# A down-projection as seven block products, each summed wholly in PSUM, in place of tile-by-tile sums in SBUF

## The reference, cut to what matters

```python
hn = rms_norm(h, ffn_norm_w)
g, val = jnp.split(hn @ w_up, [D_FF], axis=-1)
g_conv = causal_dwconv(g_hist, ffn_conv_w) + ffn_conv_b
y = h + (jax.nn.silu(g_conv) * val) @ w_down
```

## Time and profile before

| what | us |
|---|---|
| median of 3 runs | 1752.43 |
| lowest, highest | 1752.2, 1753.86 |
| span of the profiled execution | 1750.6 |
| down-projection, first to last matmul start | 1497.7 to 1746.6 |

### The profile page before, as it was taken

One profiled execution on the slowest core, in us unless ns is written; L12 is line 12 of the kernel. 1 busy time (PEld: TensorE's weight loads), 2 busy tenths in 40 slices (PEclk: granted clock), 3 DMA queues, 4 the chain that ended last, 5 costly groups with the idle time before them and its releaser, 6 DMA issues.

```text
span 1750.6 us, 31893 instructions
## 1 busy us (share of the span) xinstructions
PE 1683.5 (96%) x11519; PEld 1618.8 (92%) x11519; DVE 1242.1 (71%) x1957; ACT 695.0 (40%) x1054; POOL 881.0 (50%) x466
## 2 busy tenths in 40 slices
PE   7999999999999989999799998999999999999999
PEld 5858999999999878889799998999999999999999
DVE  5569999999899645565543378877677776655555
ACT  4755552232111377776212335434444444211110
POOL 2504762455786556664221225766666666733331
PEclk9999999999999889999999999999999999999999
DMA  5321112111776242322343312222222222622222
GB/s 197 84 70 37 36 48 86 61 49 61 267 236 207 75 140 77 87 85 85 110 135 132 143 64 80 88 75 83 72 77 79 72 94 86 231 97 96 96 77 97
DMA packets 66978, 178.32 MB, mean 102 GB/s; under 512 B 15386, under 2 KB 15514, under 8 KB 66762
## 3 DMA queue, kind: packets, MB, share of 16 engines
q1 hardware_dynamic: 56786, 140.91, 24.3%
q10 hardware_dynamic: 9392, 32.10, 4.8%
q0 software_dynamic: 720, 4.29, 0.6%
HBM read 141.79 MB, written 35.58 MB: 101 GB/s over the span
## 4 chain that ended last, share of the span: by engine, by line
PE 76%; DVE 11%; ACT 3%; POOL 3%; issue 3%; SPq 2%; DMA 1%; DVEq 0%; ACTq 0%; POOLq 0%
PE PS L667 17%; PE PS L1079 15%; PE PS L1143 11%; PE PX L1079 6%; PE PS L1002 5%; PE PS L1047 5%; PE PS L955 4%; PE PX L1143 4%; PE PS L925 2%; DVE S L2158 2%; DVE M L2156 2%; PE PX L938 2%; PE PS L983 2%; DVE LD L2138 2%; PE PS L770 1%
## 5 line engine op out<-in xcount | busy, mean ns | idle before, releaser
L667 PE MATMUL PS<-XH,WHI 128*128 128x346 f32 (+1 forms) x984 | 322.1, 327 | 5.8 <-POOL WLO L1778 4.5
L667 PE MATMUL PS<-XL,WHI 128*128 128x346 f32 (+1 forms) x984 | 318.6, 324 | 0.0
L667 PE MATMUL PS<-XH,WLO 128*128 128x346 f32 (+1 forms) x984 | 318.0, 323 | 0.0
L1778 POOL TENSOR_TENSOR WLO<-WRAW,WHI 128x1024 fp32r<-128x1024 f32 x58 | 143.4, 2472 | 296.8 <-ACT WHI L1171 296.7
L2158 DVE MATCH_REPLACE8 S<-M,S 128x1024 f32<-128x1024 f32 (+3 forms) x224 | 206.1, 927 | 0.0
L667 PEld LDWEIGHTS PS<-XH,WHI 128*128 128x128 f32 x984 | 186.9, 190 | 15.7 <-issue 8.8
L2156 DVE MAX8 M<-S 128x8 f32<-128x1024 f32 (+3 forms) x224 | 200.8, 932 | 0.4
L667 PEld LDWEIGHTS PS<-XL,WHI 128*128 128x128 f32 x984 | 187.1, 190 | 0.0
L667 PEld LDWEIGHTS PS<-XH,WLO 128*128 128x128 f32 x984 | 187.1, 190 | 0.0
L2432 DVE TENSOR_TENSOR HY<-HY,PS 128x344 f32<-128x344 f32 x198 | 100.9, 514 | 79.2 <-PE PS L1143 79.2
L1143 PE MATMUL PS<-FH,DLO 128*128 128x344 f32 x396 | 126.7, 320 | 0.0
(11 more groups left out here) (369 smaller groups left out, 4818.5 us busy)
## 6 DMA issues: line engine op xcount, KB each, us to landing
WRAW<-wtiles SPq DMA_DIRECT2D x49, 512.0 KB, 3.7
KR<-cache_k SPq DMA_DIRECT2D x64, 256.0 KB, 3.1
RING<-cache_v SPq DMA_DIRECT2D x64, 256.0 KB, 3.0
ffn_act<-TG ACTq DMA_DIRECT2D x22, 516.0 KB, 2.7
FRAW<-ffn_act SPq DMA_DIRECT2D x11, 1032.0 KB, 7.0
RAWG<-wtiles SPq DMA_DIRECT2D x22, 512.0 KB, 3.7
RAWV<-wtiles SPq DMA_DIRECT2D x22, 512.0 KB, 4.4
DRAW<-wdown SPq DMA_DIRECT2D x11, 1024.0 KB, 4.9
```

What stands on the lines that cost most here:

```text
L667: last = nc.tensor.matmul(PS[b][:, c, 0:n], w[b][:, kk, :], x[:, kk, t0 + c * n:t0 + (c + 1) * n], start=(kk == 0 and p == 0), stop=(kk == ...
L1778: nc.gpsimd.tensor_tensor(WLO[b][:, :, :], WRAW[b][:, :, :], WHI[b][:, :, :].bitcast(F32), ALU.subtract).then_inc(w_lo[b], 1)
```

## The change

The down-projection is now seven block products as well. Both halves of the hidden width (11 tiles each, k = 0 to 10), both halves of the 1032 rows (516 columns, as 2 x 258) and both halves of the 8 output tiles make 2x2 blocks. The order of the products is `GROUPS`; step n = 11 g + k is one tile of one product, 77 in all.

- SP loads all 22 activation tiles once into `KA` and `KB` (528 KB each, `ACTS` groups them by semaphore), the weights in 99 quarters of 128x512 (256 KB) into eight buffers `WQ` in turn, and the residual into `HY`, in one written-out order. Quarter j waits until the low part of the step that used quarter j - 8 is done. P5 takes three quarters a step, P7 two, P6 none, the others one.
- ScalarE casts per step the activation half (`x_high`, after TensorE finished step n - 3) and the weights (`w_high`). GpSimd makes all weights' low parts (`LOW_POOL` = 77), VectorE the activations' (`x_low`), and VectorE also the sums of weights (two per step of P5, kept in `S2`; one for P3 and P7) two steps ahead, and the sums of activations T1 to T4 (11 each).
- TensorE keeps the sum of a product over its 11 steps in PSUM, four pairs of banks. At the first step of a product each pair waits for VectorE's add of the product before it (`add_product`, at position 11 g + 1 of VectorE's order, the last thing there); P5 is copied from PSUM to SBUF by ScalarE first (`keep_p5`) and used twice. P6, P7 and P4 go on in the banks without a restart.
- The last tile's work of the up-projection lies among the first steps. The PSUM banks of the up-projection are laid out anew; its products are the same.

```diff
-        FRAW = [at("FRAW0", [P, 2, NY], oh1 + 8192), at("FRAW1", [P, 2, NY], o7 + 2 * HB)]
-        DRAW = at("DRAW", [P, 2, D], oh1)
+        KA = at("KA", [P, KS, NY], oh1)
+        KB = at("KB", [P, KS, NY], o7)
+        S2 = at("S2", [P, KS, 512], oh1 + 4 * KS * NY)
...
+        GROUPS = ("P2", "P5", "P3", "P1", "P6", "P7", "P4")
+        STEPS = KS * len(GROUPS)
+        PARTS = {"P2": ((0, 0),), "P5": ((0, 1), (KS, 1), (KS, 0)), "P3": ((0, 0),), "P1": ((KS, 0),), "P6": (),
+                 "P7": ((KS, 1), (KS, 0)), "P4": ((0, 1),)}
+        LOW_POOL = STEPS
...
+            def quarter(j):
+                n, f, h = QUARTERS[j]
+                if j >= 8:
+                    sp.wait_ge(*low_ready(QUARTERS[j - 8][0]))
+                sp.dma_start(WQ[j % 8][:, :], wd_d[f, :, h * 512:(h + 1) * 512]).then_inc(quarter_in(j)[0], 16)
...
+            for p, js, fs in (("P1", (0, 1), (0, 1, 2, 3)), ("P5", (2,), (4, 5, 6, 7)), ("P6", (3,), ()), ("P2", (4, 5), ()),
+                              ("P7", (6, 7), ()), ("P3", (), (8, 9, 10)), ("P4", (), ())):
+                sp.wait_ge(mm[1], place(NF // 2 - 1, 1, p))
...
+            for j, fs in ((8, (11, 12)), (9, (13, 14)), (10, (15, 16)), (11, (17, 18)), (12, (19, 20)), (13, (21,))):
+                quarter(j)
+                for f in fs:
+                    activation(f)
+            for x in range(2):
+                for j in range(14 + 3 * x, 17 + 3 * x):
+                    quarter(j)
+                for m in range(4 * x, 4 * x + 4):
+                    residual_back(m)
+            for j in range(20, len(QUARTERS)):
+                quarter(j)
...
+            def down(n):
+                g, k, r = n // KS, n % KS, n % 3
+                pe.wait_ge(d_xl, n + 1)
+                pe.wait_ge(*low_ready(n))
+                new = GROUPS[g] in ("P2", "P5", "P3", "P1")
+                for m in range(4):
...
+                    elif k == 0:
+                        pe.wait_ge(*((d_p5, m + 2) if GROUPS[g - 1] == "P5" else (d_add, 4 * (g - 1) + m + 1)))
+                    for q, (w, x) in enumerate(((DWH[r], DXH[r]), (DWH[r], DXL[r]), (DWL[r], DXH[r]))):
+                        for c in range(2):
+                            last = nc.tensor.matmul(PAIRS[m][:, c, :], w[:, m * P:(m + 1) * P], x[:, c * YQ:(c + 1) * YQ],
+                                                    start=new and k == 0 and q == 0, stop=k == KS - 1 and q == 2,
+                                                    skip_group_check=True)
...
+            for n in range(7, STEPS):
+                x_high(n)
+                w_high(n)
+                if n == 2 * KS + 1:
+                    for m in range(4):
+                        keep_p5(m)
...
-            def act_low(i, b):
-                pool.wait_ge(f_hi, i + 1)
-                nc.gpsimd.tensor_tensor(FL[b][:, :, :], FRAW[b][:, :, :], FH[b][:, :, :].bitcast(F32), ALU.subtract).then_inc(f_lo, 1)
+            def w_low(n):
+                pool.wait_ge(d_wh, n + 1)
+                nc.gpsimd.tensor_tensor(DWL[n % 3][:, :], w_source(n), DWH[n % 3][:, :].bitcast(F32),
+                                        ALU.subtract).then_inc(d_wlp, 1)
...
+            def weight_sums(n):
+                for j in js:
+                    dve.wait_ge(*quarter_in(j))
+                if g == "P5":
+                    nc.vector.tensor_tensor(w[1], w[0], w[1], ALU.add).then_inc(d_sum, 1)
+                    dve.wait_ge(d_sum, w_sums(n) - 1)
+                    nc.vector.tensor_tensor(S2[:, k, :], w[1], w[2], ALU.subtract).then_inc(d_sum, 1)
...
+            def position(n):
+                x_low(n)
+                if n >= LOW_POOL:
+                    w_low(n)
+                if n + 2 < STEPS:
+                    weight_sums(n + 2)
+                for what, n0 in (("T1", 6), ("T2", 3 * KS), ("T3", 4 * KS), ("T4", 6 * KS - 2)):
+                    if 0 <= n - n0 < KS:
+                        act_sum(what, n - n0)
+                if n % KS == 1 and n > KS:
+                    add_product(n // KS - 1)
```

More of the change, by code:

```diff
@@ L43 @@
 Y0 = NMETA - C0
[L44 to L45 removed]
+NY = 1032
+YH = NY // 2
+YQ = YH // 2
 NH, HD = 8, 64
@@ L603, in _ @@
                         up_weights(i, a, which)
[L605 to L609, removed]
-            def down_weights(i):
-                sp.dma_start(DRAW[:, :, :], wd_d[ds(2 * i, 2), :, :].rearrange("a p m -> p a m")).then_inc(d_raw, 16)
-            def residual_back(m):
-                sp.dma_start(HY[m][:, :], hx_d[m, :, :]).then_inc(x_in[m], 16)
@@ L630, in _, with activation @@
-            down_weights(1)
-            def down_loads(i, b):
-                sp.wait_ge(f_lo, i - 1)
-                activations(i, b)
-                sp.wait_ge(d_lo, i)
-                down_weights(i)
-            for i in range(2, NF // 2):
-                down_loads(i, i % 2)
+            def activation(f):
+                a, i = f % 2, f // 2
+                sp.wait_ge(slab_out[a], (112, 128)[a] + 16 * (i + 1))
+                t, k = (KA, f) if f < KS else (KB, f - KS)
+                sp.dma_start(t[:, k, :], act_d[f, :, :]).then_inc(acts_in(f)[0], 16)
@@ L1156, in _ @@
+            for n in range(STEPS):
+                down(n)
         @block.scalar
@@ L1988, in _ @@
             times_rms(NF // 2 - 1, 0)
-            act_low(0, 0)
-            weight_low(0, 0)
+            for n in range(5):
+                w_low(n)
             times_rms(NF // 2 - 1, 1)
-            with pool.Fori(0, NF // 4) as j:
-                for b in (1, 0):
-                    act_low(2 * j + 2 - b, b)
-                    weight_low(2 * j + 2 - b, b)
+            for n in range(5, LOW_POOL):
+                w_low(n)
         @block.vector
@@ L2494, in _ @@
             up(NF // 2 - 1, 0)
-            up(NF // 2 - 1, 1, True)
-            conv(NF // 2 - 1, 1)
-            for m in range(KD):
-                dve.wait_ge(x_in[m], 64)
-                down(0, NCH * m, NCH * m + NCH)
-                if m == 2:
-                    times_val(NF // 2 - 1, 1)
-            with dve.Fori(1, NF // 2) as i:
-                down(i)
+            conv(NF // 2 - 1, 0)
+            times_val(NF // 2 - 1, 0)
+            add(NF // 2 - 1, 1, "G1")
+            x_low(0)
+            add(NF // 2 - 1, 1, "V2")
+            x_low(1)
+            add(NF // 2 - 1, 1, "G2")
+            gates(NF // 2 - 1, 1)
+            x_low(2)
+            conv(NF // 2 - 1, 1, lambda: x_low(3))
+            x_low(4)
+            x_low(5)
+            times_val(NF // 2 - 1, 1)
+            for n in range(6, STEPS):
+                position(n)
+            add_product(len(GROUPS) - 1)
 def _constants():
```

245 lines of the change are left out of this document (159 added, 86 removed).

## The result

The changed kernel takes 1756.78 us (median of 18 runs, 1751.63 to 1760.43), the kernel before 1752.87 us (18 runs, 1747.4 to 1757.18). The ratio is 1.0023, 95% interval 1.0014 to 1.0033: **slower by 0.2%**, where 0.5% faster was forecast. The profiled execution took 1759.62 us by itself, with a span of 1757.8.

A forecast was written before the change was run, and what follows sets the result against it. TensorE's down-projection matmuls, running without idle time, were taken as the bound. Terms -28.9 + 11 + 2.5 + 2 + 1 + 3.4 = -9.0 us took 1752.4 to 1743.4 us; own range 1736 to 1750, with rivals 1727 to 1753.

The forecast's parts named there:

- TensorE's work: Down-projection: 1848 matmuls of 258 columns at 119.1 ns take 220.1 us instead of 249.0, so -28.9 us.
- first boundary: P2 to P5: TensorE's step 11 waits for P2's adds, behind sums needing quarters 20 to 22; +11 us (5.4 to 15).
- the clock behind it: After the first boundary's gap TensorE runs 5.4 us at 0.55 of the pace; +2.5 us, bounds 0 and 5.
- P5's own loop: In P5, releasing and reloading a third quarter takes 3.26 us a step against 2.86; +2 us (0 to 8).
- P5 to P3: At step 22 VectorE's eight adds, 4.9 us, and two low parts against two steps of cover; +1 us (0 to 2).
- four other boundaries: At steps 33, 44, 55, 66 VectorE's chain takes 3.8 us against 2.86; 4 x 0.85 = +3.4 us (0.2 to 4).
- the 1537.6 for quarter 22: First boundary: landing time of quarter 22, taken between estimates of 1536.1 and 1538.9 us.
- SP's stop: SP waits before activation 21 until tile 21 is written, by 1514 or so; costs nothing, its queue being behind.
- The rate of the DMA: First boundary: a full DMA moves 409 GB/s by a profile row, preferred to the skill's 358; 3.16 MB take 7.7 us.
- Rival (b): In P5 quarters land late, 6.1 us, making the loop 4.8 us a step; kernel slower at 1760.8 us; chance 0.14.
- The end: After the last matmul: add 0.69 for 0.51 us, half the output bytes in the last transfers; 0 change.
- The chances: Whole kernel: faster by over 0.2% (below 1748.9 us) 0.82, same 0.06, slower 0.12.

The follow-up runs named there:

- e5: Changed kernel with a product's adds right behind x_low at boundaries and P5's second four adds spread over positions 27 to 30; 1740.83 us, 0.9941 of the kernel before.
- e1: Changed kernel with residual rows 4 to 7 loaded behind quarter 45 instead of quarter 19; 1755.28 us, 1.0017 of the kernel before.
- e2: Changed kernel with P2's four adds at VectorE's position 12 ahead of the weight sums for step 14; 1750.08 us, 0.9983 of the kernel before.

## Why the prediction was wrong, point by point

The chain of waits was the forecast's, each pause near where it was named; what failed were three terms of the sum, and all three were forecast too small: the pace of a matmul, the landing of quarter 22 and the adds of P5. The sizes added up to 13.2 us too little. The forecast length is 249.0 - 9.0 = 240.0 us, the measured one 253.2.

| term of the prediction | forecast | measured | off |
|---|---|---|---|
| TensorE's work, 1848 matmuls | 220.1 | 224.7 | +4.6 |
| first boundary | 11 | 14.4 | +3.4 |
| the clock behind it | 2.5 | 2.4 | -0.1 |
| P5's own loop | 2 | 1.9 | -0.1 |
| P5 to P3 | 1 | 5.0 | +4.0 |
| four other boundaries | 3.4 | 3.9 | +0.5 |
| not accounted for | | 0.9 | +0.9 |

- **TensorE's work** failed by the step "so 258 columns take 119.1 ns". It is a slope between two rows of two different stages, carried to a third, and it had no bounds in the sum, although the prediction itself said what 5 ns are worth. A product after a pause took 32.1 us, 121.6 ns by 264. Of that, 120.5 ns are the pace without a pause (e5), 2.6 us over the forecast in 1848; the rest, 2 us, I put down to the refilling behind eight pauses (0.2 each), for which there was no term at all. There is no one pace for a shape to carry over: 260 columns took 119.1 to 120.5 ns in the up-projection, and 258 take 119.5, 120.0 or 121.9 here, by the buffer.
- **The first boundary** was right in place and chain: adds behind sums for step 14 behind quarters 20 to 22. e1 and e2 take away one link each and the pause shrinks by 3.5 and 5.9 us. The step that failed is the 1537.6 for quarter 22, 39.9 us behind the first matmul. It landed 43.9 us behind it (1545.2 against 1501.3), 4.0 later. The 1537.6 is the middle of two estimates, of which the first has only 3.16 MB in front of the quarter. The second counts every byte of the queue, and it was the right one: loads land one behind the other from 1489 on, with no gap. Taking the middle cost 1.3 us. The other 2.5 are the rate: 22.9 MB took from 1484.3, SP's first issue, to 1545.2, less the 2.4 that are not transfer, 58.5 us or 391 GB/s, where the forecast took the 409 of one window of 5 us. The chain behind the landing took 0.2 more (2.9), and step 10 ended 0.8 later than forecast: 3.4. The low part of step 12 did end 1.5 us behind TensorE's last matmul, with sums that had waited for late quarters, and not 0.3 ahead of step 10's end; in a queue with this backlog that moved nothing. At 14.4 the term lies inside its own bounds (5.4 to 15).
- **SP's stop** ahead of activation 21 lasted until 1523.1, not 1514, as the write of tile 21 took 6.5 us to land in the full queue; it cost nothing, as the prediction says, since the loads issued before it went on landing until 1527.6.
- **The rate of the DMA.** The Trainium skill ("SBUF — State Buffer", "A bandwidth-pool intuition that's wrong") has about 358 GB/s between HBM and a core. Here the rows show 390 to 408 for sixty microseconds, so a row was rightly taken in its place, if one that stood at the top of its range.
- **The clock** was right for the first gap: pairs 0.43 us apart for 5.7 us. The bound "with two such gaps, 5" was the case: the pause at step 24 lost another 1.7, counted above with P5 to P3.
- **P5's own loop** was right (0.76, 0.47 and some of 0.1 to 0.2). Rival (b), the slower outcome, forecast 1760.8 with quarters that land late all through P5; the time came near it (1756.8) by another way. By the rows behind 1555 the DMA is at 59% and P5 runs without long pauses, so (b) is refuted as a mechanism. (Its landing for no change is 4.4 us by its own loop, 3.5 + 4.4 over two steps, and not 4.7.)
- **P5 to P3** failed by "two steps of cover". VectorE began its eight adds at 1586.77, when TensorE had 4.5 us of work left ahead of step 24 and not two steps (5.7). The adds took 7.05 us and not 4.9, and step 24's low part 0.7 behind them: 3.32 us of waiting and 1.7 of half clock. Its upper bound of 2 was wrong too. e5, which spreads four of the adds, brings the pause to 0.89, and shows this to be the cause.
- **Other boundaries** were right (0.85 forecast, 0.97 measured; the prediction's own terms, 3.8 less 2.86, give 0.94). That they can be had for nothing by putting the adds ahead of the sum was not seen; e5 shows it.
- **The end** is 3.3 us from the last matmul's end to the end of the span, where it was 3.6: right at 0, near enough.
- **The chances**: 0.82 on faster rested on a sum of -9 with an own range of 14 us. All three terms that failed came out larger than forecast, and the pace was not in the range at all. A pause also brings refilling and half clock with it, so such errors go the same way; that was not priced.

## What to carry to other kernels

When work is cut in favour of a tighter schedule, the gain (28.9 us here, 24.3 measured) is certain and the pauses are not: price each pause with its refilling and its clock, count every byte that stands ahead of a transfer in its queue, at the rate that the full queue holds for as long as that, and give the main term bounds when its rate comes from another loop. On an in-order engine put what frees the bottleneck (here the adds out of PSUM) ahead of anything that waits for a transfer, and spread bulk work that nobody waits for; that, with the loads in order of due times and an aligned start, turned +0.2% into -1.05%. Work may belong on a slower engine if it waits for less there: GpSimd's low parts of 1.3 to 1.6 us beat VectorE's of 0.69 by 8.9 us.

## What was not expected of the hardware

- Matmuls of one shape, at the same granted clock, go at a pace that depends on the buffers they read: 119.5, 120.0 or 121.9 ns for 258 columns, in a cycle of three steps with the three buffers of the ring. In the mean over the ring it is 118.7 ns for 256 columns, 120.5 for 258 and 121.5 for 260, about 0.7 ns a column, where 260 to 344 columns gave 0.44 across two stages. A start at a multiple of 16 bytes gives 0.5 ns in the mean (1.4 in one buffer, -0.2 in another). What it is in a buffer is open.
- A pause of TensorE of 0.97 us costs 1.20.
- With the DMA full at some 400 GB/s, a quarter of 256 KB takes a median of 8.3 us from issue to landing (3.0 in an emptier queue). The loads of SP's queue land in the order of issue, each behind the last by the time of its own bytes, so a load that is freed earlier in such a queue does not land earlier unless fewer bytes are issued ahead of it.
